# Dividing the probabilities on GpSimd, and keeping the mixed values on chip with features on partitions

## The reference, cut to what matters

```python
def _window_attention(q, k, v, sink):        # 8 heads, 128-token blocks, keys of the 3 nearest blocks
    ...
    p = jnp.exp(s - m)
    denom = jnp.sum(p, axis=-1, keepdims=True) + jnp.exp(sb - m)
    o = jnp.einsum('bnhgqk,bnkhd->bnqhgd', (p / denom).astype(v.dtype), vw)
def _mixers(hn, w_in, g_out_a, g_out_b, sink_a, rpb_b, w_out):
    ...
    oa = _window_attention(qa, ka, va, sink_a)
    ob = _neighbourhood_attention(...)       # 8 heads, softmax over a 2-D neighbourhood with a bias
    merged = jnp.concatenate([_rmsnorm(oa, g_out_a), _rmsnorm(ob, g_out_b)], axis=-1)
    return jnp.einsum('bse,ed->bsd', merged, w_out)
x = x + _mixers(_rmsnorm(x, g_attn), ...)
h = _rmsnorm(x, g_ffn)
x = x + _expert_choice_ffn(h, ...)           # 16 experts, each takes its best tokens
```

## Time and profile before

| | us |
|---|---|
| median of 3 runs | 2483.69 (2483.33 to 2484.32) |
| the profiled execution, its own time | 2484.71 |
| its span | 2482.9 |
| TensorE busy | 2434.5 (98%) |
| VectorE busy | 1673.5 (67%) |
| ScalarE busy | 1456.5 (59%) |
| GpSimd busy | 163.7 (7%) |

### The profile page before, as it was taken

The page is one execution under the profiler, slowest core; times in us unless marked ns, Lnnn a source line. Parts: engine busy times, 40 slices in busy tenths (PEclk is TensorE's granted clock), DMA queues, the critical chain, the costliest instruction groups (busy, mean ns, idle before and its releaser), DMA issues.

```text
span 2482.9 us, 43086 instructions
## 1 busy us (share of the span) xinstructions
PE 2434.5 (98%) x16395; PEld 2178.7 (88%) x16395; DVE 1673.5 (67%) x2432; ACT 1456.5 (59%) x2050; POOL 163.7 (7%) x172
## 2 busy tenths in 40 slices
PE   9999999999889999999999999999999999999997
PEld 7888877777579989899998989999998989999896
DVE  6355278854776767676666767666676767666677
ACT  4332189977555656556565656555565655656574
POOL 0000000000010101101010100101010110101010
PEclk9999999999989999999999999999999999999998
DMA  7353255354376767767676767767676776767696
GB/s 250 123 177 113 62 163 202 122 186 154 111 286 224 260 224 258 240 241 247 234 248 233 250 234 248 256 230 251 223 259 226 256 244 238 251 230 253 228 325 222
DMA packets 104549, 545.29 MB, mean 220 GB/s; under 512 B 11344, under 2 KB 19920, under 8 KB 54800
## 3 DMA queue, kind: packets, MB, share of 16 engines
q1 hardware_dynamic: 97072, 518.19, 59.6%
q0 software_dynamic: 7392, 25.96, 4.5%
HBM read 503.21 MB, written 40.89 MB: 219 GB/s over the span
## 4 chain that ended last, share of the span: by engine, by line
PE 69%; DVE 1%; DMA 1%; ACT 1%; issue 0%; POOL 0%; SPq 0%; DVEq 0%; ACTq 0%
PE ex_gate_ps L2043 16%; PE ex_up_ps L2043 16%; PE ex_gate_ps L2045 7%; PE ex_up_ps L2045 7%; PE ex_down_ps L2058 2%; PE ex_down_ps L2062 2%; PE ex_down_ps L2059 2%; PE ex_down_ps L2060 2%; PE ex_down_ps L2063 2%; PE ex_up_ps L2058 2%; PE ex_up_ps L2062 2%; PE ex_up_ps L2063 2%; PE ex_up_ps L2060 2%; PE ex_up_ps L2059 2%; DMA fi_x<-acc_scratch 1%; PE ex_turn_ps L2011 0%
## 5 line engine op out<-in xcount | busy, mean ns | idle before, releaser
L1879 DVE TENSOR_TENSOR ex_w_lo<-ex_w,ex_w_hi 128x2048 fp32r<-128x2048 f32 x384 | 879.8, 2292 | 440.5 <-ACT ex_w_hi L1775 437.1
L1775 ACT ACTIVATE ex_w_hi<-ex_w 128x2048 fp32r<-128x2048 f32 x384 | 733.4, 1910 | 208.7 <-PE ex_down_ps L2063 106.8
L2043 PE MATMUL ex_gate_ps<-ex_xt,ex_w_hi 128*128 128x384 f32 x2048 | 591.8, 359 | 0.7 <-DVE ex_xt L1885 0.7
L2043 PE MATMUL ex_up_ps<-ex_xt,ex_w_hi 128*128 128x384 f32 x2048 | 592.1, 359 | 0.0
L2045 PE MATMUL ex_up_ps<-ex_xt,ex_w_lo 128*128 128x192 f32 x2048 | 512.7, 250 | 0.0
L2045 PE MATMUL ex_gate_ps<-ex_xt,ex_w_lo 128*128 128x192 f32 x2048 | 512.7, 250 | 0.0
L2045 PEld LDWEIGHTS ex_gate_ps<-ex_xt,ex_w_lo 128*128 128x128 f32 x2048 | 391.1, 191 | 0.6
L2045 PEld LDWEIGHTS ex_up_ps<-ex_xt,ex_w_lo 128*128 128x128 f32 x2048 | 391.2, 191 | 0.0
L2043 PEld LDWEIGHTS ex_gate_ps<-ex_xt,ex_w_hi 128*128 128x128 f32 x2048 | 384.5, 188 | 1.6 <-issue 1.0
L2043 PEld LDWEIGHTS ex_up_ps<-ex_xt,ex_w_hi 128*128 128x128 f32 x2048 | 384.5, 188 | 0.0
L1797 ACT ACTIVATE ex_up_low<-ex_up_ps 128x384 f32<-128x384 f32 x128 | 62.9, 492 | 207.8 <-PE ex_up_ps L2045 207.8
(11 more groups left out here) (310 smaller groups left out, 4012.3 us busy)
## 6 DMA issues: line engine op xcount, KB each, us to landing
ex_w<-in_w_experts SPq DMA_DIRECT2D x384, 1024.0 KB, 4.8
pj_w<-in_w_in SPq DMA_DIRECT2D x54, 512.0 KB, 3.7
pj_xr<-in_xt SPq DMA_DIRECT2D x12, 512.0 KB, 6.0
o_scratch<-ld_out SPq DMA_DIRECT2D x24, 256.0 KB, 4.6
at_bias<-in_near_bias SPq DMA_DIRECT2D x4, 1536.0 KB, 8.8
q_p<-in_x SPq DMA_DIRECT2D x12, 512.0 KB, 4.5
acc_scratch<-k_p SPq DMA_DIRECT2D x12, 512.0 KB, 5.4
h_scratch<-q_p SPq DMA_DIRECT2D x12, 512.0 KB, 3.0
```

Source lines behind the costliest of these rows:

```text
L1775: act.activation(w_hi[:, c % SLOTS, :], w[:, c % SLOTS, :], ACT.Copy).then_inc(hi_w, 1)
L1879: dve.tensor_tensor(w_lo[:, c % SLOTS, :], w[:, c % SLOTS, :], w_hi[:, c % SLOTS, :].bitcast(F32), ALU.subtract).then_inc(lo_w, 1)
L2043: nc.tensor.matmul(out[:, b, 0:2 * CAP], w_hi[:, slot, f], xt[:, k, :, :].rearrange("p h c -> p (h c)"), start=k == 0, stop=False)
```

## The change

In `attend`, VectorE takes the reciprocals one step after the scores (`INVERT`), and GpSimd multiplies the probabilities by them in place, one instruction for each of the two heads of a unit; the flips wait for GpSimd (`shared_out`) and move to step u-3, the products to u-4. The mixed values are copied from PSUM by VectorE over the unit's own queries (`queries`), features on partitions, in step u-5. The copies by ScalarE (L820), the turning back (L943), the scaled product (L890), the stores to DRAM and the loads from it are gone. There are 8 buffers of probabilities for 4, 4 score banks for 3, 2 for 1 of the mixed values, and 2 bias buffers for 3. The drain has six steps; in it ScalarE and VectorE take the high and low part of tile 0 from SBUF and split four chunks of weights. The rows of `w_out` and its gains are reordered on the host to match.

In `mix`, the parts of every tile come from the query buffers by three strided pieces (`Mixed.parts`). The norm is applied behind the projection: each tile's two groups of heads are projected into banks of their own, and two scaled adds (`add`, parts A and B) put them into the residual sum. The sums of squares run down the partitions: ScalarE squares, GpSimd adds chunks in two instructions a tile, and TensorE sums with a column of ones, once for two tiles (`tally`). The diff, cut to what the prediction speaks of:

```diff
+    FIRST_LO, HI = 6, 4
+    def __init__(self, keep, lows, rows, sb, sem):
+        late, v_rows = keep.w_late, keep.v.sample[:].rearrange("p t c -> p (t c)")
+        self.w = [rows[:, j, :] for j in range(self.FIRST_LO)] + [v_rows, keep.k.sample[:, self.HI, :]]
+        self.w_lo = [lows[:, j, :] for j in range(self.FIRST_LO)] + [late[:, self.HI + 1, :], late[:, self.HI, :]]
+        self.w_hi = [late[:, j, :] for j in range(self.HI)]
...
+class Mixed:
+    PARTS = 1 + 2
+    def __init__(self, q):
+        self.q = q
+    def parts(self, t, dst):
+        rows, tile = slice(0, P), self.q.at(slice(0, P), slice(0, QA), t * P, P)
+        pieces = [(dst[:, 0:QA, :], tile)]
+        g, first = divmod(t, G_TILES)
+        strips = self.q.at(rows, slice(QA, DT), g * GROUP, GROUP).rearrange(
+            "p j (s r c) -> p j s r c", s=STRIPS, r=Q_ROWS)
+        into = dst[:, QA:DT, :].rearrange("p j (r s c) -> p j r s c", r=2, s=STRIPS)
+        return pieces + [(into[:, :, r, :, :], strips[:, :, :, 2 * first + r, :]) for r in range(2)]
...
-        PROBS, STATS, BIASES, V_SLOTS, SCORES = 4, 8, 3, 2 * len(V_TILES), 3
+        PROBS, STATS, BIASES, V_SLOTS, SCORES = 8, 8, 2, 2 * len(V_TILES), 4
...
-        FLIP, WEIGH, OUT, STEPS = 2, 4, 4, N + 4
+        INVERT, FLIP, WEIGH, OUT = 1, 3, 4, 5
+        STEPS = N + OUT + 1
+        def queries(v, rows):
+            b, pair, _ = units[v]
+            if b.window:
+                return keep.q.at(rows, pair, b.tile * P, P)
+            return keep.q.at(rows, QA + pair, b.kind * GROUP + b.strip * P, P)
...
+            for step in range(len(blocks) + 2):
+                if step < len(blocks):
+                    b = blocks[step]
+                    if not b.window and b.number + BIASES < len(near_start):
+                        sp.wait_ge(added, 2 * PAIRS * (step + 1))
                         load_bias(b.number + BIASES)
+                bi = step - 2
+                if bi < 0:
+                    continue
+                sp.wait_ge(kept, PAIRS * (bi + 1))
...
+        @block.gpsimd
+        def _(pool):
+            for v in range(N):
+                b, r = units[v][0], v % STATS
+                pool.wait_ge(inverted, v + 1)
+                for h in range(2):
+                    p = probs[:, (2 * v + h) % PROBS, 0:b.keys]
+                    pool.tensor_scalar(p, p, rden[:, r, h:h + 1], None, ALU.mult).then_inc(shared_out, 1)
...
-                v = u - WEIGH + 1
-                if 0 <= v < N:
-                    act.wait_ge(weighed, v + 1)
-                    if v >= 2:
-                        act.wait_ge(o_turned, v - 1)
-                    act.activation(o_turn[:, v % 2, :], mixed_ps[:, 0:P], ACT.Copy).then_inc(o_copied, 1)
...
+                    act.wait_ge(kept, PAIRS * (FIRST_TILES + 1))
+                    for dst, src in mixed.parts(0, lead.m_hi):
+                        act.activation(dst, src, ACT.Copy).then_inc(lead.hi_m, 1)
+                if N <= u < N + LEAD_SPLITS:
+                    split(u - N)
...
+                if 0 <= u - INVERT < N:
+                    v, r = u - INVERT, (u - INVERT) % STATS
...
-                if u >= OUT:
-                    v, r = u - OUT, (u - OUT) % STATS
...
-                    dve.tensor_tensor(dst, own,
-                                      rden[:, r, :].unsqueeze(2).broadcast_to([P, 2, HD]),
-                                      ALU.mult).then_inc(scaled, 1)
...
+                if 0 <= u - OUT < N:
+                    v = u - OUT
+                    dve.wait_ge(weighed, v + 1)
+                    dve.tensor_copy(queries(v, slice(0, P)), mixed_ps[v % 2][:, 0:P]).then_inc(kept, 1)
+                if u == N:
+                    dve.wait_ge(lead.hi_m, Mixed.PARTS)
+                    for (dst, src), (hi, _) in zip(mixed.parts(0, lead.m_lo), mixed.parts(0, lead.m_hi)):
+                        dve.tensor_tensor(dst, src, hi.bitcast(F32), ALU.subtract).then_inc(lead.lo_m, 1)
+                if N <= u < N + LEAD_SPLITS:
+                    j = u - N
...
-                        pe.wait_ge(exped, 2 * v + h + 1)
+                        pe.wait_ge(shared_out, 2 * v + h + 1)
...
-                if u >= OUT:
-                    v = u - OUT
-                    pe.wait_ge(o_copied, v + 1)
-                    if v >= 1:
-                        pe.wait_ge(scaled, v)
-                    turned = [nc.tensor.transpose(out_ps[:, h, 0:HD], o_turn[ROWS[h], v % 2, :],
-                                                  ident[ROWS[h], ROWS[h]]) for h in range(2)]
-                    turned[1].then_inc(o_turned, 1)
...
+            for t in range(TILES):
+                own = squares[:, t % 2, :, :].rearrange("p (l j) c -> p l j c", l=2)
+                pool.wait_ge(mixed_squared, Mixed.PARTS * (t + 1))
+                pool.tensor_tensor(own[:, :, 0:2, :], own[:, :, 0:2, :], own[:, :, 2:4, :], ALU.add).then_inc(paired, 1)
+                pool.wait_ge(paired, t + 1)
+                if t >= 2 * PAIR:
+                    pool.wait_ge(tallied, (t - 2 * PAIR) // PAIR + 1)
+                pool.tensor_tensor(partial[:, t % (2 * PAIR), :, :], own[:, :, 0, :], own[:, :, 1, :],
+                                   ALU.add).then_inc(folded, 1)
...
+            def square_mixed(t):
+                if t >= 2:
+                    act.wait_ge(folded, t - 1)
+                for dst, src in mixed.parts(t, squares[:, t % 2, :, :]):
+                    act.activation(dst, src, ACT.Square).then_inc(mixed_squared, 1)
+            def take_root1(i):
+                act.wait_ge(tallied, i + 1)
+                if i:
+                    act.wait_ge(refined1, REFINE * i)
+                act.activation(rt1[:], ss1, ACT.Sqrt, bias=eps[:], scale=1.0 / HALF).then_inc(root1, 1)
             def raise_m(n):
...
+                if n >= 2:
+                    act.wait_ge(projected, projected_with(n - 2, B, 1))
+                for dst, src in mixed.parts(n, m_hi[n % 2]):
+                    act.activation(dst, src, ACT.Copy).then_inc(hi_m, 1)
...
-                    for k in range(2):
-                        c = slice(k * HALF, (k + 1) * HALF)
-                        act.activation(merged[:, c], o[n % 2][:, c], ACT.Copy,
-                                       scale=rs1[:, k:k + 1]).then_inc(normed1, 1)
...
+                if s + 3 < TILES:
+                    square_mixed(s + 3)
...
+            def add(t, part):
+                i, col = t // PAIR, 2 * (t % PAIR) + part
+                if part == A:
+                    dve.wait_ge(x_in[t % 2], 16 * (t // 2 + 1))
+                    if t >= 2:
+                        dve.wait_ge(x2_out[t % 2], 16 * (t // 2))
+                        dve.wait_ge(turned2, 2 * (t - 1))
                 for k in range(2):
                     c = slice(k * HALF, (k + 1) * HALF)
...
+                    dve.wait_ge(projected, projected_with(t, part, k))
+                    if part == B:
+                        dve.wait_ge(summed, summed_with(t, A) - 1 + k)
+                    dve.scalar_tensor_tensor(out=x2[t % 2][:, c], in0=bank_of(t, part, k)[:],
+                                             scalar=rs1[:, i % 2, col:col + 1],
+                                             in1=(x if part == A else x2)[t % 2][:, c],
+                                             op0=ALU.mult, op1=ALU.add).then_inc(summed, 1)
...
+                if s % 2 == 0 and s < TILES:
+                    invert1(s // 2)
...
+                if t < LAST:
+                    scale_h(t)
+                    search(s, 1)
+                    if n < TILES:
+                        lower(n)
+                    add(s, A)
...
+            def tally(i):
+                pe.wait_ge(folded, PAIR * (i + 1))
+                for t in range(PAIR * i, PAIR * (i + 1)):
+                    for part in (A, B):
+                        col = 2 * (t % PAIR) + part
+                        last = nc.tensor.matmul(ss1[:, col:col + 1], partial[:, t % (2 * PAIR), part, :], ones[:],
+                                                start=True, stop=True)
+                last.then_inc(tallied, 1)
...
+                    if s % 2 and s + 2 < TILES:
+                        tally((s + 1) // 2)
```

More of the change, by code:

```diff
@@ L720, in attend @@
         flipped = keep.flipped
-        o, stored = lead.out, lead.stored
-        o_turn = sb("at_o_turn", [P, 2, P])
+        mixed = Mixed(keep.q)
         neg_top, sums, rden = (sb(f"at_{n}", [P, STATS, 2]) for n in ("neg_top", "sums", "rden"))
@@ L1012, with mix @@
 LOGITS = slice(P, P + EXPERTS)
-def mix(nc, d, route, shared, lead):
+def mix(nc, d, keep, route, shared, lead):
     ctx = ExitStack()
@@ L1344, in open_tile @@
-            def open_tile(tiles):
-                halves = [slice(k * HALF, (k + 1) * HALF) for k in range(2)]
-                for j in tiles:
-                    out, start, stop = (A_BANKS if j < 4 else B_BANKS)[0], j % 4 == 0, j % 4 == 3
-                    pe.wait_ge(hi_w, j + 1)
```

(28 more changed lines are left out.)

455 lines of the change are left out of this document (155 added, 300 removed).

## The result

| | before | after |
|---|---|---|
| median, us | 2484.01 (2483.33 to 2484.51, 4 runs) | 2514.18 (2513.79 to 2516.15, 4 runs) |
| ratio | | 1.0123, 95% interval 1.0106 to 1.0141 |
| the profiled execution | 2484.71, span 2482.9 | 2513.79, span 2511.6 |

The change makes the kernel 1.2% slower. The forecast was 2479.0, in a range of 2466 to 2494. It is rival (a) that happened.

What follows compares the result with a forecast made beforehand. TensorE's program order was taken to bound attention and `mix`, VectorE's close behind. Terms -6.7 + 3.4 + 1.2 - 3.3 - 1.0 + 1.3, plus 0.4 for clock, gave -4.7 us: 2479.0 us, range 2466 to 2494.

Steps and rivals of the forecast that it cites:

- rival (a): Attention: GpSimd's divides become the bound, from 1.0 us a divide; 2506 us at 1.29 us a divide; chance 0.12.
- the price of a divide: Attention, GpSimd, 384 columns: between a memset's 0.47 us and a two-tensor product's 1.01; 0.74 taken, 1.5 a unit, hidden.
- Turning back goes: Attention, TensorE: two loads fewer save 0.07 us a unit over 96 units, -6.7 us, between -3 and -20.
- Drain: Last scores to first matmul of `mix`: 8.39 us becomes 11.8, VectorE's row longest, +3.4 us, between +1 and +6.
- Opening: Tile 0 of `mix`: VectorE's splits and low part behind ScalarE's squares, 12.1 us becomes 13.3, +1.2, between 0 and +3.
- Tile 1 and tiles 1 to 8: `mix`: tile 1's wait for `merged` goes, -3.3 us; tiles 1 to 8 trade turning `merged` for the tally, -1.0.
- Tiles 9 to 11: `mix` tiles with the search: VectorE's extra add makes TensorE wait, +1.3 us, between 0 and +4.
- Clock: Longer drain: TensorE's clock may fall where it idles, +0.4 us added to the sum.
- Rival (b): Attention: TensorE's pauses are not fixed, the whole 0.21 us a unit goes, -20 for -6.7, 2466 us; chance 0.15.
- Rival (c): `mix`: VectorE takes over, small transpose 0.5 us late in eight tiles, drain +5, clock +2: 2487 us; chance 0.18.
- The rule that was cited for the price: GpSimd in attention: about 1.8 cycles an element at 1.2 GHz, so a divide 0.58 us before its fixed cost.
- The rule that spoke against the change: VectorE with two SBUF inputs and GpSimd reading SBUF exclude each other; opening splits up to 1.3 us later, once or twice.

Runs made afterwards that it cites:

- experiment 2: Changed kernel with GpSimd's divide as a product of two tensors, the reciprocal spread along the columns (the cheap divide): 2484.13 us, ratio 0.9998.
- experiment 9: Against experiment 2: opening squares and tally later, squares before tile 1's high part, two or three drain splits for four: 2483.48 us (two), 2481.96 (three).
- experiment 6: Against experiment 2: opening squares moved behind the weights' splits and tile 1's high part, tally at the end of tile 0: 2482.48 us, ratio 0.9994.
- experiment 1: Changed kernel without GpSimd's divides, probabilities left undivided, flips waiting for the exponentials: 2483.96 us, ratio to before 0.9999.
- experiment 3: Against experiment 2: one GpSimd product for both heads of a unit instead of two: 2484.56 us, ratio 1.0005.
- experiment 5: Two kernels: changed kernel dividing only half the columns, 2483.83 us; experiment 2 with an equally long spare product before each divide (doubled), 2570.78 us.
- experiment 7: Against experiment 2: GpSimd instead of VectorE makes the low part of tile 0 in the drain: 2484.20 us, ratio 1.0001.
- experiment 8: Against experiment 2: the edits of experiment 6 and experiment 7 together, and two weight splits in the drain for four: 2486.00 us, ratio 1.0010.

## Why the prediction was wrong, by its own steps

**The step that failed** is the price of a divide: "above it is a product of two tensors ... 1.01 us" and "I take the middle, 0.74 us, 1.5 a unit, as one tensor is read and one written; it is then hidden". The row was not an upper bound. It is another form, and the form that the change uses takes 1.25 us (2.5 ns a column and 0.3 us fixed, from 1249 and 764 ns for 384 and 192 columns). The two rows were taken as ends because the operation reads more than a memset and less than a product; on this engine the number of tensors read does not order the forms. With 1.25 in its place, the prediction's own chain (two a unit against 2.02 us) gives rival (a), and experiment 2 shows that nothing else of the change costs these 30 us. Its sentence "it decides from 1.0 us a divide" held on both sides: 0.76 and 0.83 us are hidden, 1.25 and 2 x 0.78 are not. Its chance of 0.12 was too low for a threshold that sat on the edge of its own bounds, and the range left it out.

**The size of (a)** was 2506, with a dearer divide of 1.29 us, and the kernel took 2514.2. The rival counted only the 48 units of 384 keys. The narrower ones pay too: two divides of 256 columns are 1.85 us, and such units come every 1.80 us (7.20 for four), against 1.5 to 1.6 (6.23 for the same four) with the cheap divide. The right sum was the one over all widths, 204.8 us, for a stage that then lasts 203.0.

**The rest of the sum**, read in the kernel with the cheap divide:
- Turning back goes: -6.7 forecast, -4.7 measured. The term that was too large is the 0.07 us a unit. Twelve full units in a row (the 65th to the 77th scores) take 24.40 us where they took 25.00 (432.36 to 456.76, before 435.88 to 460.88), 0.05 a unit, and 4.7 us over 95 units is 0.05 too. The deeper pipeline with its longer start was in the diff (`FLIP` 3, `WEIGH` 4, `SCORES` 4) and not in the sum, but it costs nothing: the scores of the seventh unit come 8.35 us after the first (315.55), before 8.58 (315.56). The first line is of the kernel before, the second of the cheap kernel, each behind the 24 loads of six units:

```profile
324.14 0.30 PEld L922 LDWEIGHTS at_score<-k_s,q_s 64*128 64x128 f32 x4 [0.17 <-issue]
323.90 0.30 PEld L916 LDWEIGHTS at_score<-k_s,q_s 64*128 64x128 f32 x4 [0.17 <-issue]
```

- Drain +3.4: +3.3, for the reason given: VectorE ends last, 11.06 us after the last scores, and its copies queue behind the splits. The splits are the smaller part of it: with two of the four taken out (experiment 9) it gave back 0.8 us.
- Opening +1.2: +1.9. The late start of the splits was in the sum; their collision with GpSimd's adds was left to a rule and not priced. Experiment 6 takes both away and gets 1.8 us back.
- Tile 1 and tiles 1 to 8: -4.3 forecast, -3.0 measured. The stall is gone, and nearly all of the gain is there. The tally's eight loads take 0.97 us, not 0.9 (1.09 in the opening tile), tiles go by turns of 13.4 and 14.0 (13.2 and 13.9 forecast), and tiles 2 to 8 thus give nothing of the 1.0 forecast.
- Tiles 9 to 11: +1.3, measured +1.0.
- Clock, +0.4: 0.72 between 524 and 530 us in the kernel after, behind a pause of TensorE of 1.65 us in the drain, and back at 1.00 in the opening tile; 1.00 all through the drain in the trace of the cheap kernel.
- Of the 1.4 us that the cheap kernel has gained when the lists are made (691.31 for 692.75), 1.0 is lost again behind them. That is in the expert layers, which were not edited; what loses it was not settled.

So with a cheap divide the change would have been worth nothing, and the forecast of 2479 would have been 5 us too low, inside its range. Rival (b) is refuted by 2.02 us a unit. Rival (c) has its parts (+3.3 in the drain, splits blocked in the opening) but not its wait in each tile.

The rule that was cited for the price (the Trainium skill, GPSIMD Engine Reference, Elementwise side-by-side cycle accounting) gave an estimated 0.58 us before the fixed cost. The row says 1.25 us with some 0.3 fixed, and 2.5 ns a column at that rule's 1.2 GHz is 3.0 cycles, not 1.8. The measurement decides. The rule that spoke against the change (the Trainium skill, SBUF — State Buffer, Who interferes with whom) is borne out where VectorE reads two tensors of SBUF: 4.02 us for two splits that take 2.48 without GpSimd, 3.32 for 1.36. It is borne out in attention too, where the inputs are PSUM and SBUF and VectorE keeps its 556 ns.

## What to carry to other kernels

Where work moves to an engine that was idle, sum that engine's own work over the whole stage, with every width, against the stage's length, and give a form that no row shows an upper bound well above its dearest neighbour. On GpSimd, write a multiply by a per-partition value as a product of two tensors with the value spread along the columns: 0.83 us for 1.25. And work that is hidden by TensorE in the steady state can still cost in the drain of a pipeline, where copies queue in order behind it. Before two drains are compared, look at the granted clock of each.

## What the runs showed of the hardware that was not expected

- GpSimd's `tensor_scalar` on float32 is slower (1.25 us for 128 x 384) than its product of two whole tensors (0.99), and with a constant about as slow (1.17). A copy takes 0.50.
- A product with one operand spread by a zero stride is faster (0.82) than one with two whole tensors (0.99). From 384 and 192 columns (826 and 505 ns) it is 1.67 ns a column.
- Independent GpSimd instructions overlap by some 0.04 us: 0.784 us from start to start, 0.82 us each.
- VectorE instructions with two SBUF inputs and GpSimd's hold each other up: 4.02 us for 2.48 and 3.32 for 1.36 on VectorE, 1.60 for 0.73 and 1.74 for 1.30 on GpSimd. With one input from PSUM VectorE shows nothing of it, even with GpSimd never idle.
- The granted clock of the drain differs between traces with nearly the same program there. It fell (0.50 to 0.79 over the last 3 us) in the kernel after and in experiments 1, 3, 5 (both kernels), 7 and 8, and stayed at 1.00 in experiments 2, 6 and 9. TensorE's longest pause in the drain was 1.65 us in the kernel after, 1.78 in experiments 7 and 8 and 3.31 in the doubled kernel of experiment 5; in the others it was 1.28 or 1.29, whether the clock fell or not, so the pause alone does not tell. Each kernel has one trace; how its other executions went is not known.
